# A pair of experts laid over the four 32-partition groups of SBUF, in a two-block transformer kernel on one core

## What is computed

```python
def hier_moe(h, ...):
    # each of the 512 tokens goes to 2 of the 8 experts of one of 4 groups: 1024 rows over 32 experts
    ...
    def expert_block(args):
        xb, e = args
        return (jax.nn.silu(xb @ w_gate[e]) * (xb @ w_up[e])) @ w_down[e]    # 1024 -> 256 -> 1024
    y_rows = lax.map(expert_block, (x_blocks, block_e)).reshape(R, D)
    y_rows = y_rows * row_w[:, None].astype(y_rows.dtype)
    out = jnp.zeros((T + 1, D), y_rows.dtype).at[row_token].add(y_rows)[:T]
```

## Time and profile before

| what | value |
|---|---|
| median of 3 executions | 1301.31 us (1301.28 to 1301.44) |
| the profiled execution, its own time | 1302.32 us |
| its span | 1300.0 us |
| granted TensorE clock over the span | 0.994 |
| PE busy | 1267.6 us, 98% |
| DVE busy | 613.1 us, 47% |
| the mixture in the trace | about 1045 to 1300 us |

### The profile page before, as it was taken

The page is one execution under the profiler, slowest core; times in us unless marked ns, Lnnn a source line. Parts: engine busy times, 40 slices in busy tenths (PEclk is TensorE's granted clock), DMA queues, the critical chain, the costliest instruction groups (busy, mean ns, idle before and its releaser), DMA issues.

```text
span 1300.0 us, 18634 instructions
## 1 busy us (share of the span) xinstructions
PE 1267.6 (98%) x6670; PEld 968.7 (75%) x6670; DVE 613.1 (47%) x1162; ACT 460.4 (35%) x770; POOL 535.5 (41%) x685
## 2 busy tenths in 40 slices
PE   8999999999999999999999999999999999999986
PEld 6767777787888888888888788777888875555552
DVE  4868768725542422222225765757243265222225
ACT  5657534435434324133144534145322210000102
POOL 4633323334555655555545664424644211121100
PEclk9999999999999999999999999999999999999999
DMA  7422222112334433434333333312426989999995
GB/s 221 107 65 56 66 58 66 50 49 81 98 96 113 131 97 97 130 98 129 97 98 114 97 93 85 83 49 67 128 81 268 362 323 394 424 421 424 424 423 240
DMA packets 212157, 211.38 MB, mean 163 GB/s; under 512 B 31903, under 2 KB 193425, under 8 KB 200817
## 3 DMA queue, kind: packets, MB, share of 16 engines
q1 hardware_dynamic: 203104, 200.25, 45.8%
q0 software_dynamic: 5184, 8.29, 1.7%
q10 hardware_dynamic: 3796, 1.86, 0.5%
HBM read 205.76 MB, written 16.78 MB: 171 GB/s over the span
## 4 chain that ended last, share of the span: by engine, by line
issue 39%; POOL 31%; PE 26%; DMA 1%; DVE 1%; POOLq 0%; ACT 0%; SPq 0%; DVEq 0%; ACTq 0%
POOL wlo L661 31%; PE bank L2287 8%; PE bank L2304 4%; PE bank L1915 3%; PE bank L1917 3%; PE bank L1916 3%; PE side L1945 2%; DMA y<-y_rows 1%; PE bank L1956 1%; DMA y_rows<-xe,tabi 1%; PE side L1917 1%; PE side L1915 1%; PE side L1916 1%; PE side L2203 1%; PE bank L2419 0%
## 5 line engine op out<-in xcount | busy, mean ns | idle before, releaser
L661 POOL TENSOR_TENSOR wlo<-raw,whi 128x256 fp32r<-128x256 f32 x644 | 498.2, 805 | 524.4 <-ACT whi L785 524.2
L1916 PE MATMUL bank<-actB_lo,whi 128*128 128x512 f32 x608 | 236.7, 389 | 0.0
L1915 PE MATMUL bank<-actB_hi,whi 128*128 128x512 f32 x576 | 227.7, 395 | 0.5 <-POOL wlo L661 0.5
L1917 PE MATMUL bank<-actB_hi,wlo 128*128 128x512 f32 x576 | 224.4, 390 | 0.0
L785 ACT ACTIVATE whi<-raw 128x1024 fp32r<-128x1024 f32 x161 | 169.0, 1051 | 151.8 <-PE bank L1917 124.9
L1915 PE MATMUL bank<-actA_hi,whi 128*128 128x512 f32 x400 | 157.3, 393 | 0.6 <-DVE actA_lo L1201 0.6
L1916 PE MATMUL bank<-actA_lo,whi 128*128 128x512 f32 x400 | 156.1, 390 | 0.0
L1917 PE MATMUL bank<-actA_hi,wlo 128*128 128x512 f32 x400 | 156.1, 390 | 0.0
L2287 PE MATMUL bank<-gu,xeT 128*64 128x256 f32 x1088 | 127.7, 384 | 4.7 <-issue 2.2
L1916 PEld LDWEIGHTS bank<-actB_lo,whi 128*128 128x128 f32 x608 | 114.2, 188 | 24.1 <-issue 1.0
L1915 PEld LDWEIGHTS bank<-actB_hi,whi 128*128 128x128 f32 x576 | 108.1, 188 | 25.9 <-issue 2.3
(11 more groups left out here) (433 smaller groups left out, 1653.0 us busy)
## 6 DMA issues: line engine op xcount, KB each, us to landing
dn<-in_w_exp_down SPq DMA_DIRECT2D x32, 1024.0 KB, 16.0
raw<-in_w_in SPq DMA_DIRECT2D x57, 512.0 KB, 3.8
gu<-in_w_exp_gate SPq DMA_DIRECT2D x28, 1024.0 KB
gu<-in_w_exp_up SPq DMA_DIRECT2D x28, 1024.0 KB
raw<-in_w_up SPq DMA_DIRECT2D x32, 512.0 KB, 3.9
raw<-in_w_down SPq DMA_DIRECT2D x32, 512.0 KB, 3.6
raw<-in_w_out SPq DMA_DIRECT2D x16, 512.0 KB, 3.7
raw<-in_w_in SPq DMA_DIRECT2D x16, 256.0 KB, 3.1
```

The costliest lines, as they stand in the source:

```text
L661: ins = nc.gpsimd.tensor_tensor(wlo[:, slot, at], raw[:, slot, at], whi[:, slot, at].bitcast(F32), ALU.subtract)
L1915: mm(b[:, :], w_hi, hi[:, k, :], start=first, stop=False)
L1916: mm(b[:, :], w_hi, lo[:, k, :], start=False, stop=False)
L1917: ins = mm(b[:, :], w_lo, hi[:, k, :], start=False, stop=last)
```

## The change

Each expert of a pair now sits on two groups of 32 partitions of `xe` and of the row lists, one in each half: expert 0 of the pair on partitions 0 to 31 and 64 to 95, expert 1 on 32 to 63 and 96 to 127. The PSUM banks of gate, up and down stay as they were (expert h on 64h to 64h+63), and so do all matmuls; the transposes of `turn_rows` write their columns in the old order. What crosses between the two layouts (y, and the lists) goes through VectorE in four pieces of 32 partitions instead of one instruction of 128. The order of ranks within the 64 places changes too.

```diff
+QUADRANTS = ((0, 0), (1, ROWS), (0, 32), (1, ROWS + 32))
+PLACES_OF = tuple((slice(32 * c, 32 * (c + 1)), slice(at, at + 32)) for c, (h, at) in enumerate(QUADRANTS))
+LAST_PLACES = PLACES_OF[-1][0]
+def by_expert(x):
+    return x.rearrange("p (h o s) -> p o h s", h=2, s=32)
...
-            ranks = const("iota")[:, 0:ROWS].rearrange("p (j b) -> p b j", b=8)
-            groups = rank_at.rearrange("p (b o) -> p b o", o=8)
-            for b in range(0, 8, 2):
-                chain(v.tensor_copy(groups[:, b:b + 2, b:8], ranks[:, b:b + 2, 0:8 - b]))
-                if b:
-                    chain(v.tensor_copy(groups[:, b:b + 2, 0:b], ranks[:, b:b + 2, 8 - b:8]))
+            ranks = const("iota")[:, 0:ROWS].rearrange("p (o e) -> p e o", e=16)
+            groups = rank_at.rearrange("p (e o) -> p e o", o=4)
+            for o in range(4):
+                if o % 2 == 0:
+                    chain(v.tensor_copy(groups[:, :, o:o + 1], ranks[:, :, o:o + 1]))
+                else:
+                    chain(v.tensor_scalar(groups[:, :, o:o + 1], ranks[:, :, o:o + 1], -1.0, float(32 * o + 15), ALU.mult, ALU.add))
...
-            chain(v.tensor_scalar(tabi[:, 1, 0:EXTRA_AT], bank[1][:, 0:EXTRA_AT], float(SKIP), None, ALU.add), S("rows_ready"))
+            for to, of in PLACES_OF:
+                ins = v.tensor_scalar(tabi[to, 1, 0:EXTRA_AT], bank[1][of, 0:EXTRA_AT], float(SKIP), None, ALU.add)
+                chain(ins, S("rows_ready") if to == LAST_PLACES else None)
...
-                chain(v.tensor_scalar(tabi[:, 0, FIRST], bank[2][:, 0:EXTRA_AT], float(SKIP), None, ALU.add), S("slots_ready"))
+                for to, of in PLACES_OF:
+                    ins = v.tensor_scalar(tabi[to, 0, FIRST], bank[2][of, 0:EXTRA_AT], float(SKIP), None, ALU.add)
+                    chain(ins, S("slots_ready") if to == LAST_PLACES else None)
...
                 for n in range(2):
                     x = xe[:, q % X_BUFS, n * L:(n + 1) * L]
-                    ins = v.scalar_tensor_tensor(x, bank[2 + n][:, :], slotv[:, 1, q:q + 1], x, ALU.mult, ALU.add)
+                    for to, of in PLACES_OF:
+                        ins = v.scalar_tensor_tensor(x[to, :], bank[2 + n][of, :], slotv[of, 1, q:q + 1], x[to, :], ALU.mult, ALU.add)
                 ins.then_inc(S("y_made"), 1)
...
-                    chain(v.tensor_tensor(tabi[rows, 1, to], slot, back, ALU.add))
-                    chain(v.tensor_copy(tabi[rows, 0, to], slot))
+                    chain(v.tensor_tensor(back, slot, back, ALU.add))
+                    for at, of_ in PLACES_OF if rows == slice(0, P) else ((LOW_ROWS, LOW_ROWS),):
+                        chain(v.tensor_copy(tabi[at, 1, to], prod[of_, 0, EVENS:EVENS + of.stop - of.start]))
+                        chain(v.tensor_copy(tabi[at, 0, to], prod[of_, 0, 0:of.stop - of.start]))
...
-                v.scalar_tensor_tensor(x, bank[2 + n][:, :], slotv[:, 1, LAST_E:LAST_E + 1], x,
-                                       ALU.mult, ALU.add).then_inc(S("last_y_made"), 1)
+                for to, of in PLACES_OF:
+                    ins = v.scalar_tensor_tensor(x[to, :], bank[2 + n][of, :], slotv[of, 1, LAST_E:LAST_E + 1], x[to, :],
+                                                 ALU.mult, ALU.add)
+                ins.then_inc(S("last_y_made"), 1)
...
-                    ins = turn(side[k // 4][:, (k % 4) * P:(k % 4 + 1) * P], xe[:, n_x, :].rearrange("s (p j) -> s j p", j=NK)[:, k, :])
+                    ins = turn(by_expert(side[k // 4][:, (k % 4) * P:(k % 4 + 1) * P]), xe[:, n_x, :].rearrange("s (p j) -> s j p", j=NK)[:, k, :])
```

## The result

The changed kernel takes 1325.7 us (median; 1322.4 to 1327.0) where the kernel before took 1301.3 beside it: a ratio of **1.018** (95% interval 1.0168 to 1.0192), 24.4 us more. 1322.7 was forecast, within 1308 to 1329. The profiled execution took 1325.0 us with a span of 1322.8, that is 22.7 and 22.8 more than the profiled one of before.

The account below looks back on a forecast made before the run. PE, busy 98% of the span, was taken as the bound, with weights second; time is lost where PE waits behind `y_of`. The terms sum to +21.4 us on 1301.3, so 1322.7 us; own range 1318 to 1329, with rivals 1308 to 1329.

Parts of the forecast that it names:

- 2 `rows_ready`: List setup on DVE: `rows_ready` follows four instructions instead of one, so the first gather comes later: +0.6 us.
- 5 `hidden(2)`, `hidden(3)`: Pieces of `y_of(1)` and `y_of(2)` delay the hidden layers that PE's transposes wait for: +3.3 and +1.5 us.
- Step 6: From `y_of(3)` on, POOL issues gathers 4.9 us later and PE waits for some: +1.2 us (0 to 3.2).
- Step 7: PE's clock falls once behind each of the stands of 4.9 and 3.3 us: +3.4 us; one fall, 1.7.
- item 8: Spare reads, issued behind `y_of(6)`, start later; PE waits 7.1 us instead of 2.2 before unit 9's gates: +4.9 us.
- Step 10: Tail: `y_of(15)` +4.8 us; last scatter lands in 5.0 instead of 7.4, -2.4; last y covered, nothing.
- first rival: Pieces of `y_of` overlap, 0.66 us apart instead of 0.78: +14.1 us, 1315.4 us; chance 0.20.
- second rival: Spare reads don't move with POOL, so a late PE meets them landed before unit 9: 1313.9 us; chance 0.14.
- Step 4: `list_overflow` takes 18 instructions instead of 10, 1.6 us, covered by DVE's wait before `y_of(1)`; otherwise up to 1.3 us.
- Balance pays: New places spread rows over more DMA engines, with pieces costing little: faster, 1297.5 us; chance 0.05.
- More is late: Gathers late in each unit with repeated clock falls, or DVE waiting on itself: beyond 1329, say 1332 us; chance 0.09.
- it does nothing: Pieces cost a quarter of the whole and rows were already spread evenly enough: 1301 us; chance 0.05.

Follow-up runs that it names:

- Experiment 4: experiment 1 with the two loops of `y_of` exchanged, so every second piece stays on the partitions of the one before: 1320.9 us, 1.0147.
- experiment 6: New lists and places without pieces: down matmuls in four column groups of 32, `y_of` and last y whole: 1304.3 us, 1.0018 of the kernel before.
- experiment 8: The kernel before with `y_of` in pieces in units 0 to 2 only: 1309.9 us, 1.0057.
- experiment 9: The kernel before with the three spare reads issued one unit earlier (also called the ninth kernel): 1302.7 us, 1.000.
- experiment 7: The kernel before with `y_of` in pieces in units 3 to 14 only: 1307.6 us, 1.0048.
- experiment 11: The changed kernel with POOL issuing gather q+4 before the wait for `y_of(q)` and scatter q, from unit 1 on: 1318.9 us, 1.0134.
- experiment 1: The kernel before with `y_of` and last y in eight pieces of 32x512, old ranks, lists and places kept: 1327.5 us, 1.0201.
- experiment 2: The changed kernel measured again, unaltered (its profile is the second profile): 1329.1 us, 1.0215 of the kernel before.
- experiment 10: The changed kernel with the three spare reads issued one unit earlier: 1318.6 us, 1.0124 of the kernel before.
- Experiment 3: experiment 1 with the last y in two whole instructions again, `y_of` of units 0 to 15 in pieces: 1324.8 us.
- experiment 12: The changed kernel with gather before scatter from unit 1 on and the spare reads one unit earlier: 1311.5 us, 1.0082 of the kernel before.

## Why the prediction was right, and where it was off

The direction, the mechanism and the places of the waits were right, all but the last y. That the sum came so close is partly luck: late gathers and the last y were put 2.4 and 3.1 us too low, the clock and the last scatter 1.4 and 2.4 us too high. By its steps, from the two profiled executions:

| step | forecast | measured |
|---|---|---|
| 2 `rows_ready` | 0.6 | 0.1 at unit 0's gates (1056.59, now 1056.71), though the first gather is issued 0.6 later; `y_of(0)` varies by 1.2 over the profiles with the old lists, so this isn't resolved |
| 3 `y_of(0)` | 4.9 | 4.8 |
| 5 `hidden(2)`, `hidden(3)` | 3.3 + 1.5 | 3.2 + 1.3 |
| 6 late gathers | 1.2 (0 to 3.2) | 3.6: 4.8, less a stall of 1.2 at 1154 to 1156 us in the kernel before |
| 7 clock | 3.4 | 2.0 (PE 4.9 late at the late lists, 7.0 at unit 1's downs), and 2.9 more in the second profile |
| 8 spare reads | 4.9 | 4.3, and 0.7 by a longer low clock |
| 9 weights | -0.8 | -0.8 |
| 10 `y_of(15)` | 4.8 | 4.7 |
| 10 last scatter | -2.4 | -4.8 |
| 10 last y | 0 | 3.1 |
| 11 transposes | 0 | 0 (1.15 us each, as before) |

The measured terms of the first profile (2.9 stands apart) add to 22.2. The last y ends 22.4 us late and the last instruction 22.8, the low clock from 1300.4 on lying between; the execution took 22.7 more. The median took 24.4 more, and the 1.7 us between the two aren't accounted for.

- **The price of a piece.** 0.78 was taken and 0.76 measured. Experiment 4 has both bounds, 0.66 and 0.76, in one row, and settles the first rival.
- **Step 6 failed in size.** It took the landing as 10.0 us after the issue, with the issue 4.9 us later. It is 11.0 in the middle units of the changed kernel. In every kernel with pieces there and POOL's old order it is 10.7 to 11.3, with the old places too, and in the four kernels without pieces there 9.9 to 10.3 (before, experiments 6, 8 and 9); what makes this 1 us stays open. Experiments 7 and 11 show the cause as forecast (pieces ahead of POOL's issue), and 11 that POOL's order, scatter first, is part of it. The thought that gathers with rows in both halves might land sooner was wrong.
- **Step 7 counted one fall too many.** It took one behind each stand. Behind the stand of 3.6 us the clock fell in every profile with pieces in unit 0; behind that of some 3 us it fell in four of those ten (experiments 1, 2, 8 and 10), and in the profiled execution of the result it didn't. The length of the stand alone doesn't decide it: in experiment 6 it fell behind one of 1.98 us. Such falls may be part of why runs of one kernel differ, but this isn't shown: the changed kernel spread over 4.6 us, and the kernel before, without these two stands, over 0.2, 2.2, 3.5 and 4.1 us in its four measurements.
- **Step 10 failed for the last y and the last scatter.** "DVE waits longer than that for the second block" held for the scatter of 7.4 us only. The scatter of 2.6 us, taken as 5.0, brought y back sooner, and the last y took its place. These are two errors of one cause: 2.4 us too little won and 3.1 not counted. Experiment 3 shows it.
- **The scatter.** Its quick landing comes neither from balance nor from quick places: with the old places it lands after 3.0 us (experiment 1). It comes from being late enough for the weights to have landed: around its issue the queue of weights took 78% of the DMA engines' time before, nothing after the change and in experiment 1, and 17% in experiment 6, where it landed after 2.8 us. In the ninth kernel, which is no later than before, y is read back at 1274.91, as before.
- **Spare reads.** Experiments 10 and 12 take item 8 away and the time goes with it, so the second rival falls. Step 4 (longer `list_overflow`, covered if PE is late) held, and experiment 6 shows the price without the cover: 2.0 us and the fall of the clock behind it, above the 1.3 given there.
- **Balance pays:** fell, by experiments 1, 2 and 6. The share of the indirect DMAs' queue is 1.7% as in the earlier trace rows.
- **More is late, and it does nothing:** both fell. PE stands where the prediction said and behind the last y, no wait comes back in every unit, and the change costs 24.4 us.

Open: why the clock falls in one execution and not in the next behind the same stand, and how much of the 1.98 us in experiment 6 is due to its own four added copies. Single engines of the DMA were not looked at, so whether the rows are in fact more even over them isn't shown, only that no landing is sooner.

## What to carry over

An instruction on a quarter of the partitions cost what the whole costs (0.75 us for 512 columns), so a split by partitions multiplies DVE's time; then ask at each place where that engine is on the path (lists, hidden layers, the issue of the next gather, the tail), not of its mean share. Where pieces can't be avoided, let those on the same partitions follow each other, with their inputs on the same group as what they write, and issue what doesn't need the pieces ahead of them. A wait that is taken away is won only if the stream behind it has room: here 5 us won on PE were given back to the weights in full.

## What the runs showed of the hardware

- Distance between two vector instructions of 32x512: 0.66 us where the partitions stay, 0.76 where they change, and 0.76 also between two that stay but read factor and down products on other partitions than x.
- Matmuls of 32 columns in four groups run beside each other as those of 64 in two (3.64 us for 32 of them, 3.60 for 16), but going from 64 columns to 32 and back costs 0.11 us one way and 0.14 the other, 0.31 a unit with the gates behind. The Trainium skill's page "TensorEngine Tiling (Array Packing)", section "Key Properties", says that changing the tiling mode drains the engine; the two gaps agree with it, though no row shows the drain itself.
- The kernel before has a stall whose releaser the trace names only as "remote": 1.60 us in the copies of `turned`, while POOL issues the spare reads. With these issued 11 us earlier (experiment 9) it is gone, though a copy runs beside them then too. What holds DVE there stays open. The row, in the timeline of DVE in the kernel before:

```profile
1155.67 0.69 DVE L1687 TENSOR_TENSOR xeT<-side,small 128x512 f32<-128x512 f32 x1 [1.60 <-remote]
```
